# Moving every buffer behind the small ones 32 bytes further on in a hybrid decoder layer

## What is computed

```python
h    = rms_norm(x, norm_mix_pre)
proj = h @ w_in                                   # 1024 x 1792
u_pool, g_b, g_c, u_conv, q, k, v = split(proj)
y_pool = pool_mixer(u_pool, pool_w, pool_scale)   # trailing means of 2, 4, 8, 16
y_conv = g_b * causal_dwconv(g_c * u_conv, conv_w)
y_attn = swa_sink_attention(q, k, v, attn_sinks)  # 8 heads, window 128
mix  = concat(y_pool, y_conv, y_attn) @ w_o       # 1024 x 1024
x    = x + rms_norm(mix, norm_mix_post)
h    = rms_norm(x, norm_ffn_pre)
gate, val = split(causal_dwconv(h @ ffn_w_up, ffn_conv_w) + ffn_conv_b)   # 2 x 2816
ff   = (silu(gate) * val) @ ffn_w_down            # 2816 x 1024
out  = x + rms_norm(ff, norm_ffn_post)
```

## Time and profile before

| | us |
|---|---|
| median of 3 runs | 1020.34 |
| lowest, highest | 1019.39, 1020.65 |
| the profiled execution, time | 1019.89 |
| the profiled execution, span | 1018.1 |

### The profile page before, as it was taken

One profiled execution on the slowest core, in us unless ns is written; L12 is line 12 of the kernel. 1 busy time (PEld: TensorE's weight loads), 2 busy tenths in 40 slices (PEclk: granted clock), 3 DMA queues, 4 the chain that ended last, 5 costly groups with the idle time before them and its releaser, 6 DMA issues.

```text
span 1018.1 us, 11937 instructions
## 1 busy us (share of the span) xinstructions
PE 997.1 (98%) x4580; PEld 808.2 (79%) x4580; DVE 637.8 (63%) x702; ACT 408.4 (40%) x624; POOL 30.6 (3%) x82
## 2 busy tenths in 40 slices
PE   8999999999999996999999999999999999999997
PEld 7987777777888885888888888888887888888886
DVE  5636786665554588878778878878864323344454
ACT  5525444444342234444444445444433322333342
POOL 2200000000111000000000000000000000000001
PEclk9999999999999998999999999999999999999999
DMA  6520110116323110332232232222216343455553
GB/s 218 151 62 22 42 42 22 41 55 199 108 95 104 62 62 12 113 104 78 68 102 66 82 92 75 82 84 82 104 63 216 124 155 126 152 195 187 176 175 124
DMA packets 84912, 104.91 MB, mean 103 GB/s; under 512 B 3849, under 2 KB 63489, under 8 KB 84865
## 3 DMA queue, kind: packets, MB, share of 16 engines
q1 hardware_dynamic: 84737, 104.20, 31.3%
q0 software_dynamic: 128, 0.07, 0.0%
HBM read 84.33 MB, written 19.92 MB: 102 GB/s over the span
## 4 chain that ended last, share of the span: by engine, by line
PE 93%; DVE 3%; DMA 2%; ACT 1%; POOL 0%; SPq 0%; issue 0%; DVEq 0%; POOLq 0%; ACTq 0%
PE ps L1439 29%; PE ps L1441 29%; PE ps L1440 29%; PE ps L1449 1%; PE ps L1547 1%; DMA xin<-in_x 1%; PE ps L1570 1%; PE ps L1548 1%; PE ps L1556 1%; DVE r_lo L1277 1%; PE ps L1574 1%; DMA wraw<-in_w_o 1%; DMA act_in<-act_dram 0%; DVE hlo L961 0%; PE ps L1585 0%
## 5 line engine op out<-in xcount | busy, mean ns | idle before, releaser
L961 DVE TENSOR_TENSOR wlo<-wraw,whi 128x1024 fp32r<-128x1024 f32 x60 | 73.3, 1224 | 144.7 <-ACT whi L602 144.6
L602 ACT ACTIVATE whi<-wraw 128x1024 fp32r<-128x1024 f32 x60 | 63.3, 1057 | 180.2 <-PE ps L1441 176.3
L1439 PE MATMUL ps<-whi,ahi 128*128 128x512 f32 x320 | 127.7, 399 | 1.0 <-DVE alo L1238 1.0
L1441 PE MATMUL ps<-whi,alo 128*128 128x512 f32 x320 | 126.2, 394 | 0.0
L1440 PE MATMUL ps<-wlo,ahi 128*128 128x512 f32 x320 | 125.5, 392 | 0.0
L1439 PE MATMUL ps<-hhi,whi 128*128 128x512 f32 (+1 forms) x256 | 96.7, 378 | 2.1 <-DVE hlo L979 2.1
L1441 PE MATMUL ps<-hhi,wlo 128*128 128x512 f32 (+1 forms) x256 | 94.1, 367 | 0.0
L1440 PE MATMUL ps<-hlo,whi 128*128 128x512 f32 (+1 forms) x256 | 94.0, 367 | 0.0
L1441 PEld LDWEIGHTS ps<-whi,alo 128*128 128x128 f32 x320 | 60.1, 188 | 15.6
L1439 PEld LDWEIGHTS ps<-whi,ahi 128*128 128x128 f32 x320 | 60.1, 188 | 15.2 <-DVE alo L1238 1.4
L1440 PEld LDWEIGHTS ps<-wlo,ahi 128*128 128x128 f32 x320 | 60.1, 188 | 14.3
(11 more groups left out here) (196 smaller groups left out, 2109.3 us busy)
## 6 DMA issues: line engine op xcount, KB each, us to landing
wraw<-in_ffn_w_up SPq DMA_DIRECT2D x44, 512.0 KB, 5.0
wraw<-in_ffn_w_down SPq DMA_DIRECT2D x44, 512.0 KB, 3.4
act_dram<-yv SPq DMA_DIRECT2D x22, 512.0 KB, 2.6
act_in<-act_dram SPq DMA_DIRECT2D x42, 256.0 KB, 3.5
wraw<-in_w_in SPq DMA_DIRECT2D x14, 512.0 KB, 3.9
xin<-in_x SPq DMA_DIRECT2D x8, 512.0 KB, 4.4
wraw<-in_w_o SPq DMA_DIRECT2D x8, 512.0 KB, 3.2
xres<-in_x SPq DMA_DIRECT2D x8, 512.0 KB, 4.0
```

Source lines behind the costliest of these rows:

```text
L602: act.activation(hi[:, slot, :], wraw[:, base % RAW, :], ACT.Copy)\
L961: dve.tensor_tensor(lo[:, slot, :], wraw[:, base % RAW, :], hi[:, slot, :], ALU.subtract).then_inc(w_split, 1)
L1439: pe.matmul(acc, w_hi, x_hi, start=first, stop=False, skip_group_check=looped)
L1441: return pe.matmul(acc, w_lo, x_hi, start=False, stop=last, skip_group_check=looped)
```

## The change

One buffer of 8 float32 (32 bytes) that nothing uses is allocated between `small` and `gain_a`. Everything allocated after it, gain_a among it, begins 32 bytes further on. wraw, whi, wlo, cst and the small buffers stay where they were. The number, the order and the shapes of all instructions stay the same on each engine; what differs in the built program is the addresses (and the line numbers behind the new line, by one).

```diff
         neg_bias = alloc(ctx, "neg_bias", [P, NF])
         small = alloc(ctx, "small", [P, 2, 6, 4])
+        alloc(ctx, "before_gain_a", [P, 8])
         gain_a = alloc(ctx, "gain_a", [P, DM])
```

## The result

The changed kernel takes 1015.82 us (median of 12 runs, 1014.38 to 1018.49) where the kernel before takes 1021.14 us in the same runs (12 runs, 1019.39 to 1023.41). The ratio is 0.9944, with a 95% interval of 0.9933 to 0.9954: faster by 5.3 us by the medians and by 0.56% (5.7 us) by the ratio. The forecast was 16 us. The sign is right, the range (1001 to 1021) holds the time, and the size is wrong by a factor of three.

A forecast was written before the change was run, and what follows sets the result against it. PE was taken as the bound (busy 997.1 of 1018.1 us), so time is matmul count times pace. Gains 6.1 + 10.2 + 0.4 - 0.3 = 16.4 us gave a forecast of 1004.0 us, range 1001 to 1021.

The forecast's parts named there:

- It is the place of whi and wlo that costs 7 ns: Large matmuls using whi or wlo: their address alone was said to make them about 7 ns slower than 226.7 ns.
- The step that failed: All matmuls pairing whi or wlo with other operands: equal residues mod 64 would bring each slow pair to 226.7 ns.
- The term of the ring: Down ring, 960 matmuls with whi or wlo moving: 233.3 to 226.7 ns each, 6.1 us gained after a longer wait.
- the term of the projections: Projection and up projection, 1368 matmuls with whi or wlo stationary: 234.3 to 226.7 ns each, 10.2 us gained.
- The settling term: Matmuls just behind a run with whi, some 25 places: they would no longer need to settle, 0.4 us gained.
- The argument for 64 bytes: Steady paces are whole multiples of 6.67 ns, which is 64 bytes of the stream, so 64 bytes looked like the unit.
- rival 1: No change: readers collide by a larger unit than 64 bytes or by region, so time stays 1020.3 us; chance 0.22.
- Rival 3: Half: only whi's moving role is mended (1014.2 us) or only its stationary role (1010.1 us); chance 0.04.
- Rival 2: Slower: an operand at 0 mod 64 is itself slow, so 1572 fast matmuls slow down, 1031.5 us; chance 0.16.
- The 256 columns: First pass, 192 matmuls of 256 columns: agreement gains nothing and may cost 1.4 ns each, -0.3 us.
- The rule of the Trainium skill: TensorE's two read ports are independent, so the reads could not disturb each other: gain 0, time 1020.3 us.
- DMA and the first x: Two DMAs on the chain write buffers that move, first x (9.44 us) and act_in (4.55 us): 0, with +-0.5 us.

The follow-up runs named there:

- pad96: The changed kernel with 96 unused bytes in place of 32 before gain_a; 1006.04 us, ratio 0.9853.
- w_behind: The kernel before with whi and wlo allocated behind the small buffers, at 288 mod 512 like the other product operands; 1005.26 us, ratio 0.9838.
- group runs: Programs of matmuls only, not the layer, in groups at set distances between moving and stationary operand; 226.7 ns at distance 0 with 512 float32r columns.

## Why the prediction was right or wrong

- **What bounds the kernel** was right. PE's matmuls at different paces were the thing to see, and waits did not eat the gain: in pad96, with 15 us less, PE is busy for 98% of the span as before, and its listed waits are 17.0 us in all against 15.1, with 1.3 of the difference in the wait for hrow_a at the start.
- **"It is the place of whi and wlo that costs 7 ns"** was right in size, and right that a place relative to the others is the cause. Mended at the right distance, it gives 15 to 17 us (w_behind 0.9838, pad96 0.9853), so the forecast's sum of 16.4 was the price of the mismatch within the intervals of these runs.
- **The step that failed** is "No pair differs mod 64 any more. If agreement is what counts, every slow pair falls to 226.7 ns". Agreement mod 64 is not what counts: the unit is 256 bytes. The pairs went from a distance of 160 to one of 192 mod 256 with whi stationary, and from 96 to 64 with whi moving. The term of the ring, 6.1 us, was really 4.0 (4.3 by the steps, less 0.3 for the longer wait for alo); the term of the projections, 10.2 us, was really 1.1 to 1.3. The settling term, 0.4, was about 0: h2hi past w2hi has a mean step of 228.2 ns before and 228.4 after, since slow matmuls still stand before it. In pad96, where it could settle, it is 226.6.
- **The 5 us are no part of the forecast's gain.** They are what the distances 192 and 64 happen to give against 160 and 96. That the sign came out right, and that the time fell into a range which reached up to 1021 only to take in "no change", is in good part luck.
- **The trace of before already spoke against 64 bytes.** Mod 64 the up projection and the ring are at the same distance (32 and -32), and yet they ran at 234.3 and 233.3 ns. Either the role matters or the unit is larger; the prediction read both paces and counted them as one class.
- **The argument for 64 bytes** in rival 1 was weak and carried too much. The steady paces of 226.7 and 233.3 ns were whole multiples of 6.67 ns over their periods. So is the ring's in the kernel after (228.9 x 3 = 686.7 = 103 of them), with a period of 256 bytes. What the pace is counted in does not say at which distance the two reads repeat.
- **Rival 1** ("just two classes of large matmuls, agreeing mod 512 and not agreeing mod 64, so it cannot tell these apart") named the gap in the evidence, and had the right doubt with the wrong outcome: a larger unit was given as no change, though a new distance is a new pace. None of the cases had a pace that the trace did not show yet. Rival 3, half of it, came nearest: 1014.2 for the moving role alone, which is what was measured for the most part, at a chance of 0.04.
- **Rival 2** fell with the changed kernel itself, where hhi past mhi kept 226.7 ns at 0 mod 64, and again with the run in which everything moves.
- **The 256 columns** were read as evidence against a simple rule, then given 0.3 us and left. They were the only row with another column count, and the group runs show that the best distance differs by it. The term had the wrong sign for this change: from the second pair of token tiles on they step by 117.8 ns after, against 118.5 to 119.1 before, some 0.3 us with the first pair.
- **The rule of the Trainium skill** ("SBUF — State Buffer", "Who interferes with whom": TensorE with two independent read ports, waiting for no one) would make all distances equal. The group runs show 226.7 to 236.7 ns in float32r with VectorE and ScalarE idle; in float32 and bfloat16 the trace agrees with it.
- **DMA and the first x** were given 0, with +-0.5 us for the range. PE's wait for hrow_a is 0.8 us before, 2.8 after and 1.4 to 2.2 in the other four profiles of the layer. With one profile of each kernel that is no effect of the change that these runs could show, but it is wider than the 0.5.

## What to carry to other kernels

When a kernel is bound by float32r matmuls of 512 columns, read the steps between their start times by pair of buffers, and compare them with those of a pair that steps fastest. If two classes differ, work out the *distance* of the two operands and try more than one: here, buffers at equal residues mod 256 bytes in each partition were worth 1.5%, and equal residues mod 64 a third of that. With 256 columns the best distances were others, so the column count has to be the kernel's own. An alignment that two cases of a trace support fits several moduli; name them all, and price each at what it would really give, which may be a value that the trace has not shown yet.

## What was not expected of the hardware

- The pace of float32r matmuls of 512 columns with a new stationary operand each time depends on the distance of the two operands, with a period of 256 bytes: 226.7 ns at 0, 228.9 at 64, up to 236.7 at 240. With 256 columns, 113.3 ns at 64 and 192 and 120.0 at 0. With 384 columns, 173.3 at six of eight distances.
- Float32 (two rows of 429.2 ns for each matmul) and bfloat16 (215.8 ns) with 512 columns do not depend on it, at the eight distances tried.
- It takes the stream some matmuls to settle: behind a matmul of 64 columns, a group at distance 0 began with a step of 313 ns and five of 228 to 236, and then ran at 226 to 227; the mean over its 31 steps is 230.3.
- What exactly meets what is open. Of two operands in turn at different residues, no theory tried here gives the pace.
